# Seven block products instead of eight in the gate and up products of a SwiGLU FFN, fp32, on one Trainium2 core

## The reference

```
for l in range(2):
    mod = silu(c) @ ada_w[l] + ada_b[l]          # 9 vectors of 1024
    x = x + 0.5*(1+g0) * swiglu(mod0(rms(x)), ffn_w_in[l,0], ffn_w_out[l,0])
    x = x + (1+g1) * token_mixer(mod1(rms(x)), ...)
    x = x + 0.5*(1+g2) * swiglu(mod2(rms(x)), ffn_w_in[l,1], ffn_w_out[l,1])
return rms(x)

def swiglu(h, w_in, w_out):                      # w_in 1024 x 5632, w_out 2816 x 1024
    gate, up = split(h @ w_in, 2)
    return (silu(gate) * up) @ w_out
```

## Time and profile before

| what | value |
|---|---|
| median of 3 runs | 1584.64 us (1584.37 to 1584.91) |
| the profiled execution, its own time | 1584.97 us |
| its span, first to last instruction | 1583.2 us |
| TensorE busy | 1541.5 us (97%) |
| weight loads busy | 1343.5 us (85%) |
| VectorE busy | 595.7 us (38%), 1139 instructions |
| ScalarE busy | 238.5 us (15%) |
| HBM read | 280.10 MB, 178 GB/s over the span |
| mean granted TensorE clock | 0.987 of 2.4 GHz |

### The profile page before, as it was taken

The page is one execution under the profiler, slowest core; times in us unless marked ns, Lnnn a source line. Parts: engine busy times, 40 slices in busy tenths (PEclk is TensorE's granted clock), DMA queues, the critical chain, the costliest instruction groups (busy, mean ns, idle before and its releaser), DMA issues.

```text
span 1583.2 us, 22718 instructions
## 1 busy us (share of the span) xinstructions
PE 1541.5 (97%) x10014; PEld 1343.5 (85%) x10014; DVE 595.7 (38%) x1139; ACT 238.5 (15%) x446; POOL 75.8 (5%) x143
## 2 busy tenths in 40 slices
PE   5999999999999989999999999999999999999998
PEld 4888888788888878888888888878888888888887
DVE  5443435564443332232253434455633432111111
ACT  2100001532222020000030000035222201100001
POOL 7000000000000000000000000000000000000000
PEclk7999999999999999999999999999999999999999
DMA  9878877242413556667657878744341248355550
GB/s 335 287 254 276 271 253 232 86 126 87 108 29 99 200 165 199 224 202 239 213 154 259 291 251 279 236 135 127 107 107 29 55 160 259 121 170 171 156 159 28
DMA packets 306211, 282.63 MB, mean 179 GB/s; under 512 B 15368, under 2 KB 269696, under 8 KB 306112
## 3 DMA queue, kind: packets, MB, share of 16 engines
q1 hardware_dynamic: 287168, 211.12, 44.2%
q0 software_dynamic: 17952, 69.21, 11.9%
q10 hardware_dynamic: 992, 0.85, 0.2%
HBM read 280.10 MB, written 1.05 MB: 178 GB/s over the span
## 4 chain that ended last, share of the span: by engine, by line
PE 95%; DVE 2%; DMA 1%; ACT 1%; issue 0%; ACTq 0%; SPq 0%; DVEq 0%
PE ps L1284 94%; DMA arena<-in_ada_w_dram 1%; PE ps L1288 1%; DVE ada_acc L811 1%; ACTq L601 0%; ACT rs L533 0%; DVE y_m L1155 0%; ACT hT L533 0%; DVE hT L842 0%; ACT arena L533 0%; SPq L400 0%; DVE hT L845 0%; DVE arena L1189 0%; DVE arena L1194 0%; DVE ada_turn L817 0%
## 5 line engine op out<-in xcount | busy, mean ns | idle before, releaser
L1284 PE MATMUL ps<-hT,ring 128*128 128x256 f32 (+1 forms) x4000 | 894.0, 381 | 4.8 <-ACT hT L533 4.8
L1284 PEld LDWEIGHTS ps<-hT,ring 128*128 128x128 f32 (+1 forms) x4000 | 753.7, 190 | 120.9 <-issue 10.7
L1284 PE MATMUL ps<-arena,ring 128*128 128x256 f32 (+1 forms) x1568 | 356.6, 381 | 4.4 <-DVE arena L887 4.4
L1284 PEld LDWEIGHTS ps<-arena,ring 128*128 128x128 f32 x1568 | 299.4, 191 | 46.2 <-DVE arena L887 4.8
L894 DVE TENSOR_TENSOR arena<-arena,ps 128x256 f32<-128x256 f32 x85 | 35.8, 421 | 548.4 <-ACT arena L567 548.3
L811 DVE SCALAR_TENSOR_TENSOR ada_acc<-ada_stage,cond,ada_acc 128x512 f32<-128x512 f32 x231 | 173.5, 751 | 8.9 <-DMA ada_stage<-in_ada_w_dram 1.2
L567 ACT ACTIVATE arena<-ps 128x256 f32<-128x256 f32 x85 | 32.5, 383 | 820.7 <-PE ps L1284 820.7
L460 POOL DMA_DIRECT2D ada_stage<-in_ada_w_dram x66 | 49.6, 752 | 1361.9 <-DVE ada_acc L811 733.7
L1284 PEld LDWEIGHTS ps<-arena 64*64 64x64 f32 (+1 forms) x2880 | 94.1, 136 | 18.7 <-issue 8.5
L1284 PE MATMUL ps<-arena 64*64 64x64 f32 (+3 forms) x2880 | 101.6, 227 | 8.0 <-ACT arena L533 2.8
L533 ACT ACTIVATE arena<-ps 128x256 f32<-128x256 f32 (+4 forms) x96 | 42.7, 468 | 123.8 <-PE ps L1284 97.5
(11 more groups left out here) (211 smaller groups left out, 691.9 us busy)
## 6 DMA issues: line engine op xcount, KB each, us to landing
ring<-in_ffn_w_in_dram SPq DMA_DIRECT2D x176, 512.0 KB, 5.2
ada_stage<-in_ada_w_dram POOLq DMA_DIRECT2D x66, 1024.0 KB, 9.1
ring<-in_ffn_w_out_dram SPq DMA_DIRECT2D x88, 512.0 KB, 8.7
ring<-in_mix_w_in_dram SPq DMA_DIRECT2D x46, 512.0 KB, 5.1
ring<-in_mix_w_in_dram SPq DMA_DIRECT2D x12, 1024.0 KB, 5.3
ring<-in_mix_w_in_dram SPq DMA_DIRECT2D x6, 1536.0 KB, 6.4
ring<-in_mix_w_out_dram SPq DMA_DIRECT2D x8, 1024.0 KB, 5.0
arena<-in_ada_w_dram SPq DMA_DIRECT2D x6, 1024.0 KB, 18.0
```

The costliest lines, as they stand in the source:

```text
L1284: return nc.tensor.matmul(out_, lhsT, rhs, start=start, stop=stop, **kw)
```

## The change

For all chunks from 2 on (but 7, 12 and 17 in the first FFN; 77 of 88 chunks) the gate and up products are no longer 16 matmuls of 256 columns. The inner dimension is cut into two halves of four tiles, the tokens into two halves of 128, and gate and up are the two output halves. This 2x2 by 2x2 block product is done in seven block products (Strassen's, in Winograd's form), each of four matmuls with 128 moving columns: 28 matmuls of 128 columns.

- VectorE forms four sums of weight blocks (128x512 each) per chunk, two chunks ahead (`weight_sums(c + 2)`), once the weights have landed; and four sums of `hT` blocks once per FFN (`token_sums`).
- The seven results lie in two PSUM banks. ScalarE copies the first to SBUF, VectorE adds them up in four instructions (three of 128x256, one of 128x128), ScalarE applies silu to the two gate parts and VectorE multiplies as before, now from SBUF.
- VectorE does the weight sums between these additions and the multiplication of chunk c.
- The adaLN blocks become 12, 10, 8 and 2 for the four FFNs, all in chunks 2 to 19, and are summed over partitions once per FFN, within up(21).
- SBUF for the sums: `w_sums` in the arena, the token sums in `y_r` and `y_m`. The DMAs of the weights, and their sizes, stay.

```
+def units_of_chunk(l, half, c):
+    n, over = UNITS * len(ada_blocks(l, half)), ADA_END - ADA_FIRST      # 2, 20
+    done = [n * min(max(i - ADA_FIRST, 0), over) // over for i in (c, c + 1)]
+    return range(*done)
+def seven(l, half, c):
+    return c >= 2 and not (l == half == 0 and c in (7, 12, 17))
...
 # ScalarE, ffn
+                    if seven(l, half, c):
+                        ac.wait_ge(bank_ready, SEVEN_BEFORE[l, half, c] + 1)
+                        nc.scalar.activation(parts[:, 7, :], ps[:, base(c), 0:P], ACT.Copy).then_inc(first_copied, 1)
+                        ac.wait_ge(parts_ready, SEVEN_BEFORE[l, half, c] + 1)
+                        nc.scalar.activation(view(sil[:, c % 2, :], 2, P), parts[:, 0:7:6, :], ACT.Silu)\
+                          .then_inc(sil_ready, 1)
+                        continue
 # VectorE, ffn
+                    if seven(l, half, c):
+                        dv.wait_ge(gu_ready, n + 1)
+                        dv.wait_ge(first_copied, SEVEN_BEFORE[l, half, c] + 1)
+                        link(l, V.tensor_tensor(parts[:, 0:2, :], parts[:, 7:8, :].broadcast_to([P, 2, P]),
+                                                both[:, 1:5:3, :], ALU.add))
+                        link(l, V.tensor_tensor(parts[:, 2:4, :], parts[:, 1:2, :].broadcast_to([P, 2, P]),
+                                                both[:, 2:6:3, :], ALU.add))
+                        V.tensor_tensor(parts[:, 4:7:2, :], parts[:, 2:4, :], both[:, 3:7:3, :], ALU.add)\
+                         .then_inc(parts_ready, 1)
+                        free(V.tensor_tensor(parts[:, 5, :], parts[:, 2, :], both[:, 5, :], ALU.add))
+                        weight_sums(l, half, c + 2)
...
+            def weight_sums(l, half, c):
+                dv.wait_ge(*landed(l, use))
+                V.tensor_tensor(s1, a21, a22, ALU.add).then_inc(w_summed, 1)
+                V.tensor_tensor(s3, a11, a21, ALU.subtract).then_inc(w_summed, 1)
+                dv.wait_ge(w_summed, done + 1)
+                V.tensor_tensor(s2, s1, a11, ALU.subtract).then_inc(w_summed, 1)
+                dv.wait_ge(w_summed, done + 3)
+                V.tensor_tensor(s4, a12, s2, ALU.subtract).then_inc(w_summed, 1)
...
 # TensorE, up(c) of such a chunk; a.. are blocks of w_in, x.. of hT, s.. and t.. the sums
+                    def product(place, a, b):
+                        for j in range(4):
+                            last = mm(both[:, place, :], a(j), b(j), start=(j == 0), stop=(j == 3))
+                        return last
+                    product(0, a11, x11)
+                    product(1, a12, x21)
+                    pe.wait_ge(t_summed, t_sums_done(*before))
+                    product(3, a22, t4)
+                    pe.wait_ge(w_summed, summed + 2)
+                    product(2, s3, t3).then_inc(bank_ready, 1)
+                    if c == NC - 1:
+                        last_sums()
+                    pe.wait_ge(w_summed, summed + 3)
+                    product(4, s2, t2)
+                    product(5, s1, t1)
+                    pe.wait_ge(w_summed, summed + 4)
+                    product(6, s4, x22).then_inc(gu_ready, 1)
```

More of the change, by code:

```diff
@@ L127, in ada_blocks @@
     if half == 0:
[L128 to L129 removed]
+        return [(l, 2 * D + n * BLOCK) for n in range(4 if l else 0, 12)]
+    return [(l, 8 * D + n * BLOCK) for n in range(2)] + [(l + 1, n * BLOCK) for n in range(8) if l + 1 < DEPTH]
+ADA_FIRST, ADA_END = 2, 20
 def units_of_chunk(l, half, c):
[L134 to L135 removed]
+    n, over = UNITS * len(ada_blocks(l, half)), ADA_END - ADA_FIRST
[3 more added lines that the diff above has]
+    return c >= 2 and not (l == half == 0 and c in (7, 12, 17))
+SEVEN_BEFORE = {}
+for _l in range(DEPTH):
+    for _half in range(2):
+        for _c in range(NC):
+            SEVEN_BEFORE[_l, _half, _c] = sum(seven(*at) for at in SEVEN_BEFORE)
 ADA_BEFORE = {}
@@ L352, in slot_of, with t_sums_done @@
             return RING[l * USES + use][0]
+        def t_sums_done(l, name):
+            return 4 * (1 + [(None, "start"), (0, "mixer"), (0, "half 1"), (1, "mixer")].index((l, name)))
         def landed(l, use):
@@ L896, in ffn @@
+                    if c == 0:
+                        token_sums(*before)
+                    if not seven(l, half, c):
+                        weight_sums(l, half, c + 2)
                     ada_of_chunk(l, half, c)
-                    if c == NC - 3:
+                    if c == NC - 2:
                         dv.wait_ge(*PE.at(l, f"ada {half}"))
                         if half == 0:
-                            link(l, V.tensor_tensor(mod[:, 16:40], ps[:, 7, 0:24], par_a[:, R_ADA + 16:R_ADA + 40],
-                                                    ALU.add), "ada 0 read")
+                            if l:
+                                free(V.tensor_tensor(mod[:, 16:32], mod_next[:, 16:32], par_a[:, R_ADA + 16:R_ADA + 32],
+                                                     ALU.add))
+                            first = 32 if l else 16
+                            link(l, V.tensor_tensor(mod[:, first:64], ps[:, 7, 0:64 - first],
+                                                    par_a[:, R_ADA + first:R_ADA + 64], ALU.add))
@@ L913, in ffn @@
                                                      ALU.mult), "final diagonals")
[L914 to L921, removed]
@@ new lines, in weight_sums @@
+            def weight_sums(l, half, c):
+                if c >= NC or not seven(l, half, c):
+                    return
+                use, done = half * (NC + N_MIX) + c, 4 * SEVEN_BEFORE[l, half, c]
+                w = view(ring[:, slot_of(l, use), 0:2048], 8, 2, P)
+                a11, a12, a21, a22 = (w[:, k:k + 4, g, :] for g in range(2) for k in (0, 4))
+                s1, s2, s3, s4 = (w_sums[:, c % 2, n] for n in range(4))
+                dv.wait_ge(*landed(l, use))
[5 more added lines that the diff above has]
+                V.tensor_tensor(s4, a12, s2, ALU.subtract).then_inc(w_summed, 1)
@@ L1342, in up @@
                         return
+                    if seven(l, half, c):
+                        up_of_seven(c, w)
+                        return
                     for g in range(2):
@@ new lines, in last_sums @@
+                def last_sums():
+                    pe.wait_ge(hid_ready, n0 + NC - 1)
+                    blocks = len(ada_blocks(l, half))
+                    pe.wait_ge(*DV.at(l, f"ada {half} {blocks - 1}"))
+                    ada_columns(7, 0, 0, blocks, f"ada {half}")
+                    if half and l + 1 < DEPTH:
+                        pe.wait_ge(params_full, 16 * N_PARAM_DMAS * (l + 2))
+                        params("params next", 6)
+                    if half and l + 1 == DEPTH:
+                        pe.wait_ge(g_full, 16)
+                        turn(ps[:, 6, 128:136], rows_c[:, :]).then_inc(*PE.step("final column"))
```

100 lines of the change are left out of this document (61 added, 39 removed).

## The result

| | before | changed |
|---|---|---|
| median | 1584.51 us (1582.89 to 1584.91, 4 runs) | 1532.68 us (1530.60 to 1537.84, 4 runs) |
| profiled execution, its span | 1584.97, 1583.2 us | 1532.11, 1530.4 us |

The ratio is 0.968, 95% interval 0.9655 to 0.9705: 52 us faster.

What follows compares the result with a forecast made beforehand. The prediction took TensorE's own stream in the FFNs as the bound: 1584.97 - 50.4 saved in gate-up + 6 of stall = 1540.6, stated as 1540.5 us. The range was 1530 to 1561 us.

Steps and rivals of the forecast that it cites:

- The bound, and the pitch of 112 ns: FFNs: TensorE's own stream bounds the kernel; 128-column matmuls start 112 ns apart, read from a mixer run of 16 records.
- the group's mean of 122: Mixer's 128-column matmuls: busy time over count, 3.9/32 = 122 ns, set aside because it counts record tails as work.
- The sum on TensorE, 50.4 us: Gate-up of 77 chunks: 6.255 instead of 6.91 us each, 0.655 less, so 50.4 us saved.
- The added waits: TensorE's two to four new waits per chunk: priced at nothing; 26 us at the other end.
- The adaLN columns: Column sums and parameter turns moved into each FFN's last gate-up: zero on balance.
- VectorE's 5.0 us per chunk: VectorE's additions, weight sums and `hid` per seven-product chunk, with some 30 ns between instructions: 5.0 us; first FFN 93% busy.
- The landing at 10.1 us, and a wait of 1.7 us in each chunk: Weights of c+2 land 10.1 us after gate-up starts; VectorE waits 1.7 us, leaving `hid` 2.4 us spare.
- The 6 us of stall: TensorE stalls charged: 4 us in the first FFN, 2 in the second, none later; bounds 0 and 35 us.
- VectorE as the bound: Rival, first two FFNs: VectorE's work and DMA waits stall TensorE 20 to 40 us, 1565 us named; chance 0.13.
- The return trip: Rival: slot freed, weights land, sums, `hid`, down loop over two chunks; 1614 us at a 15.3 us landing; chance 0.05.
- The loads as the bound: Rival, gate-up: 128x128 weight loads at 190 ns each limit the matmuls, 3.73 us more per chunk, 1872 us; chance 0.03.
- The pitch of 122: Rival, gate-up: pitch 122 to 124 ns, seven products cost what eight did, 1579 to 1588 us; chance 0.02.

Runs made afterwards that it cites:

- two more additions: Changed kernel with two extra 128x512 VectorE additions per chunk, ahead of the multiplication, into unused memory: 1545.91 us.
- a run of its own: Changed kernel with weight sums made three chunks ahead instead of two, with a third buffer, still before the multiplication: 1977.63 us.
- the run with eight products: Kernel before, with gate and up of chunks 2 to 21 as 32 matmuls of 128 columns instead of 16 of 256, no sums: 1604.56 us.
- an overfull VectorE: Changed kernel with four extra 128x512 VectorE additions per chunk, ahead of the multiplication, into unused memory: 1595.84 us.

## Why the prediction was right, and where it was off

- **The bound, and the pitch of 112 ns.** Right. Gate-up takes 6.25 us and the pitch is 111.6 ns with operands from `hT` and the ring. Reading the run of 16 with its tail taken off was the step that decided the size of the gain: the group's mean of 122 would have given 6 us.
- **The sum on TensorE, 50.4 us.** Right: the four FFNs gave 51.0. The added waits cost nothing. That 51.0 stands so near is partly luck: 0.8 of it is the clock, and the start-up before the first FFN took 1 us more than before. The adaLN columns, priced at zero on balance, saved 0.2 to 0.4 us in the last two FFNs. But moving them made a new place at which TensorE waits for `hid`, ahead of the down part, which the prediction doesn't have; it cost 0.9 us in one profile of two.
- **VectorE's 5.0 us per chunk.** This step failed, by 16%, and with it the 345 us by which VectorE was to be busier: it was 309. The trace shows 4.31 from the first addition to the next piece of work. I had added a gap of 30 ns to each record's duration. But VectorE's records overlap where one instruction doesn't wait for the one ahead: 0.68 us long, 0.60 apart. The earlier trace rows show it too: the multiplication at 128.64 lasts 0.42 and the next starts at 128.98, 0.34 later. Counted that way, the first FFN needs 15 x 4.31 + 3 x 0.35 + 24 x 3.7 = 155 of 177 us (an estimate from these rows), 87% instead of 93%.
- **The landing at 10.1 us, and a wait of 1.7 us in each chunk.** Also off. In 58 to 230 us VectorE waited for weights six times, 10.4 us in all, and once in the window of the second FFN. The last DMA of a chunk landed after 7.5 us and not 8.9. The multiplication was then done 4.7 us before the down part in most chunks of the last three FFNs, not 2.4; in the first FFN it was 2.2 to 8.7, by how many adaLN units VectorE had to do (2.2 in the chunk shown, 132.59 against 134.82, which came late out of two). What goes with the earlier landing in the traces is the phase of the other stream. In the kernel before, GpSimd sent the 1 MB of an adaLN unit within a microsecond of the weights in most chunks, as here:

```profile
173.12 0.99 SPq L387 DMA_DIRECT2D ring<-in_ffn_w_in_dram  x2
...
173.82 0.75 POOL L460 DMA_DIRECT2D ada_stage<-in_ada_w_dram  x1 [9.88 <-DVE ada_acc L811]
174.15 1.11 SPq L389 DMA_DIRECT2D ring<-in_ffn_w_out_dram  x1
```

  After, it goes out more than 4 us behind them in 49 of the 51 chunks that have one (123.90 against 119.05 above), since the unit before it is summed later in the chunk. The last DMA of a chunk and the units land sooner, the units after 6.8 instead of 9.0 us, the first two DMAs of a chunk later, after 5.9 instead of 5.2. The chunks of one execution can be sorted by this: before, the last DMA landed after 8.8 us (median) in the 44 chunks with a unit within 1 us, after 6.0 in the 35 without a unit; in the changed kernel after 6.6 in the 49 with a unit over 4 us behind. This speaks for the phase, but it isn't shown by a run, since none changed it alone.
- **The 6 us of stall.** None came in one profile and 0.9 us in the other, which is most of the distance between 1540.5 and the 1532 to 1534 of the runs; the clock makes most of the rest. With VectorE at 87% and 12 us of waits for landings it has about one addition per chunk to spare.
- **The rivals.** VectorE as the bound: not at this load, but from two more additions on; its place (first two FFNs) was right. The return trip: its fast form shown by a run of its own; the form over two chunks, which the prediction priced, was not active and not tested. The loads as the bound: out, by the run with eight products. The pitch of 122: out.

## What to carry to other kernels

The busy time of a group divided by its count isn't the price of one instruction: take a run of equal instructions and divide the distance between starts. Before a matmul is cut into smaller ones to save some of them, the price of the cut stands alone in one run (here 0.24 us a chunk against 0.89 saved), and it was paid only because the products left out are one in eight. When work is moved to an engine that had time, ask two things apart: whether its total fits (here TensorE lost nothing that counts with VectorE busy up to about 90% of the stretch), and whether its new waits close a circle with the transfers; here a circle that closed within one chunk cost 443 us, an overfull VectorE 61. And look for the one place at which its result is wanted earliest: there the reserve ends first.

## What the runs showed of the hardware

- The fp32 matmul shows as two records; their pitch is 112 ns at 128 columns and 216 at 256 at a granted clock of 1.00, with a fresh 128x128 load for each.
- VectorE's additions of 128x512 in fp32 stand 0.60 us apart when the second doesn't wait for the first (130.24 to 130.84) and 0.72 when it does (130.84 to 131.56). The Trainium skill, VectorE: DVE Perf Modes, section on the DRAIN you can't avoid, says of a row of copies that a semaphore after each costs nothing extra; here the pair with the wait costs 0.12 us more.
- Behind an idle of 4.6 us of TensorE the clock was at 1.2 GHz for a time: the down part took 6.16 us instead of 3.62. So such a stall costs more than its length: 289 us of waits, of 4.7 us on average, made 443.
- The changed kernel's executions spread by 8 us, with the granted clock from 0.984 to 0.990. In the profiles such differences lie in how long TensorE is at 1.2 GHz at the start of the second FFN and within the mixers (298.5, 300.2 or 301.8 us for the same mixer, with 0, 3.4 or 6.8 us at that level).
